# One buffer for a weight chunk's raw words and its low half, and splits two chunks ahead

## The reference

```python
mod = silu(c) @ w_mod[l] + b_mod[l]                    # 6 vectors of 1024: shifts, scales, gates
h = rms_norm(x, g_pre_mix) * (1 + scale1) + shift1
x = x + gate1 * rms_norm(token_mixer(h, ...), g_post_mix)
h = rms_norm(x, g_pre_mlp) * (1 + scale2) + shift2
x = x + gate2 * rms_norm(square(relu(h @ w_ff1)) @ w_ff2, g_post_mlp)
```

## Time and profile before

| | |
|---|---|
| timed runs, median of 3 | 4700.61 us (4700.21 to 4706.22) |
| profiled execution, span | 4705.3 us |
| TensorE busy | 4064.1 us, 86% |
| VectorE busy | 2280.9 us, 48% |
| ScalarE busy | 1600.9 us, 34% |
| weights' low halves (VectorE, L291) | 645 x 1.225 us = 789.1 us |
| weights' high halves (ScalarE, L283) | 645 x 1.055 us = 679.5 us |
| weight loads | 645 x 512 KB, 3.2 us from issue to landing (median) |
| bytes moved by DMA | 356.36 MB, mean 76 GB/s |

### The profile page before, as it was taken

One profiled execution on the slowest core, in us unless ns is written; L12 is line 12 of the kernel. 1 busy time (PEld: TensorE's weight loads), 2 busy tenths in 40 slices (PEclk: granted clock), 3 DMA queues, 4 the chain that ended last, 5 costly groups with the idle time before them and its releaser, 6 DMA issues. The chain is left out here.

```text
span 4705.3 us, 49824 instructions
## 1 busy us (share of the span) xinstructions
PE 4064.1 (86%) x17808; PEld 2981.2 (63%) x17808; DVE 2280.9 (48%) x3743; ACT 1600.9 (34%) x2635; POOL 73.3 (2%) x62
## 2 busy tenths in 40 slices
PE   7879797978899699977978899699979876898877
PEld 5749796733488588756733487588767433685435
DVE  5756564665443444464755443444433345333263
ACT  5445333234433222253334433222222333223332
POOL 0000000010000000000010000000000010000010
PEclk9869898989999799988989999799989578897688
DMA  8305342200022122262200022122222000221001
GB/s 279 126 27 188 121 162 88 85 18 0 18 98 95 51 96 94 85 224 81 85 23 1 18 98 98 50 94 94 84 72 90 0 18 5 72 94 36 14 5 41
DMA packets 95775, 356.36 MB, mean 76 GB/s; under 512 B 11008, under 2 KB 11264, under 8 KB 94592
## 3 DMA queue, kind: packets, MB, share of 16 engines
q1 hardware_dynamic: 95616, 354.27, 21.7%
HBM read 351.08 MB, written 3.15 MB: 75 GB/s over the span
## 5 line engine op out<-in xcount | busy, mean ns | idle before, releaser
L291 DVE TENSOR_TENSOR w_lo<-w_raw,w_hi 128x1024 fp32r<-128x1024 f32 x645 | 789.1, 1225 | 958.4 <-ACT w_hi L283 956.3
L306 PE MATMUL banks<-h_hi,w_hi 128*128 128x512 f32 (+1 forms) x2808 | 1031.5, 367 | 105.3 <-PEq L499 64.1
L307 PE MATMUL banks<-h_lo,w_hi 128*128 128x512 f32 (+1 forms) x2808 | 1027.9, 366 | 0.0
L308 PE MATMUL banks<-h_hi,w_lo 128*128 128x512 f32 (+1 forms) x2808 | 1026.1, 365 | 0.0
L283 ACT ACTIVATE w_hi<-w_raw 128x1024 fp32r<-128x1024 f32 x645 | 679.5, 1055 | 789.0 <-PE banks L308 705.1
L306 PEld LDWEIGHTS banks<-h_hi,w_hi 128*128 128x128 f32 x2808 | 537.3, 191 | 201.5 <-issue 112.3
L307 PEld LDWEIGHTS banks<-h_lo,w_hi 128*128 128x128 f32 x2808 | 537.5, 191 | 89.0
L308 PEld LDWEIGHTS banks<-h_hi,w_lo 128*128 128x128 f32 x2808 | 537.1, 191 | 89.5
L1190 DVE TENSOR_REDUCE row_max<-banks 128x1 f32<-128x768 f32 (+4 forms) x288 | 192.3, 668 | 351.2 <-PE banks L1068 181.7
L1141 ACT ACTIVATE turned<-banks 128x512 f32<-128x512 f32 (+3 forms) x296 | 145.8, 493 | 513.8 <-PE banks L1100 513.1
L1100 PE MATMUL banks<-consts,weights 128*128 128x128 f32 x896 | 187.8, 326 | 127.9 <-DVE weights L1163 83.8
(11 more groups left out here) (255 smaller groups left out, 5213.4 us busy)
## 6 DMA issues: line engine op xcount, KB each, us to landing
w_raw<-in_stream SPq DMA_DIRECT2D x645, 512.0 KB, 3.2
dft_table<-in_dft SPq DMA_DIRECT2D x2, 2048.0 KB, 8.6
x<-in_x SPq DMA_DIRECT2D x1, 2048.0 KB, 11.6
out_x<-x SPq DMA_DIRECT2D x1, 2048.0 KB, 6.3
context<-in_ctx SPq DMA_DIRECT2D x1, 1024.0 KB, 4.6
ctx_kept<-context SPq DMA_DIRECT2D x1, 1024.0 KB, 3.8
rope<-in_rope SPq DMA_DIRECT2D x2, 512.0 KB, 3.6
context<-ctx_kept SPq DMA_DIRECT2D x1, 1024.0 KB, 4.8
```

The costliest lines, as they stand in the source:

```text
L291: self.nc.vector.tensor_tensor(self.lo[:, n % SLOTS], self.raw[:, n % SLOTS], self.hi[:, n % SLOTS].bitcast(F32), ALU.subtract)\
L306: self.nc.tensor.matmul(out, w_hi, x_hi, start=start, stop=False)
L307: self.nc.tensor.matmul(out, w_hi, x_lo, start=False, stop=False)
L308: mm = self.nc.tensor.matmul(out, w_lo, x_hi, start=False, stop=stop)
```

## The change

The low half of a chunk is written over the raw words it was computed from (`over`, with the other type), and the ring `lo` no longer has memory of its own. A load now waits until the products of the chunk in its slot are done, and for nothing else. ScalarE's wait for the used slot goes, because a chunk can't have landed before. `AHEAD` is 2, and SyncE loads up to the stage's end plus 4.

```diff
-AHEAD = 3
+AHEAD = 2
...
         self.raw = K.take("w_raw", [SLOTS, CHUNK * P])
         self.hi = K.take("w_hi", [SLOTS, CHUNK * P], F32R)
-        self.lo = K.take("w_lo", [SLOTS, CHUNK * P], F32R)
+        self.lo = K.over("w_lo", self.raw, F32R)
...
     def load(self, sp, n, place, step=0):
         if n >= SLOTS:
-            sp.wait_ge(self.lo_ready, step + (n - SLOTS + 1))
+            sp.wait_ge(self.chunk_used, step + self.after(n - SLOTS + 1))
...
         act.wait_ge(self.chunk_loaded[n % SLOTS], step_loads + 16 * (n // SLOTS + 1))
-        if n >= SLOTS - 1:
-            act.wait_ge(self.chunk_used, step + self.after(n - SLOTS + 1))
         self.nc.scalar.activation(self.hi[:, n % SLOTS], self.raw[:, n % SLOTS], ACT.Copy)\
             .then_inc(self.hi_ready, 1)
...
+    def over(self, name, t, dt):
+
+        self.n += 1
+        at = next(a for a, _, n in self.held if n == t.name)
+        return self.nc.alloc_sbuf_tensor_at(f"{name}_{self.n}", list(t.shape), dt, offset=at)
+
...
     def _(sp):
-        W.load_upto(sp, end_chunk + AHEAD + SLOTS)
-        W.loaded = min(W.total, end_chunk + AHEAD + SLOTS)
+        W.load_upto(sp, end_chunk + SLOTS)
+        W.loaded = min(W.total, end_chunk + SLOTS)
```

## The result

The changed kernel takes 4738.4 us (median of 4, 4734.9 to 4739.7), the kernel before 4703.3 us in the same comparison: a ratio of 1.0075, 95% interval 1.0063 to 1.0087. The change costs 35 us, where 4717 us, +16.5, had been forecast. It lies in the stated range of 4703 to 4742, near its upper end, and outside the forecast's own 4711 to 4728. The profiled execution spans 4737.0 us against 4705.3.

What follows compares the result with a forecast made beforehand. TensorE was taken to bound the weight stages, except modulation, bound by the weights' slot loop. Modulation +15, gate +1 and SyncE +0.5 gave +16.5 us on the 4705.3 us span, 4721.8; timed runs lie 4.7 lower: 4717 us, range 4703 to 4742.

Steps and rivals of the forecast that it cites:

- Place and mechanism: Modulation stages: the weights' slot loop is the limit there and gets longer by hand-over to TensorE and six matmuls.
- fixed part: Modulation slot loop: everything except a load's issue-to-landing time, 2.58 us before the change and 4.21 us after.
- main term: 22 modulation groups of four chunks go from 7.18 and 7.07 us to 7.8 us: +15 us.
- the bounds: Modulation: landing between 3.2 and 4.6 us, loop 7.41 to 8.81 us, cost +6 to +37 us.
- L: Time from a weight load's issue to its landing in modulation: 4.6 us before, taken as 3.6 us after.
- signs: Modulation: row copies 7.5 to 8.2 us apart, landings 3.2 to 3.8 us, SyncE waiting for matmuls, DMA share about 0.78.
- The lost head start: Seven chunks loaded or split before a stage become four; counted inside the first turn of the loop, nothing extra.
- Rival 1: Modulation: landing doesn't get shorter, staying at 4.6 us; +37 us there, 4739 us in all; chance 0.13.
- The other stages: Outside modulation loads stay hidden: 1 us in the 256-column gate stage, 0.5 us for SyncE at stage ends, otherwise 0.
- Rival 2: Modulation: the slot loop stays under what the DMA engines need; groups stay at 7.1 us, 4701 us; chance 0.23.
- Rival 3: Modulation: TensorE's clock falls to the lower level, groups of 12.2 us, +112 us, 4813 us; chance 0.03.
- Rival 4: Attention: the clock falls otherwise because all is shifted, 10 us either way; chance 0.05 for gain, 0.05 for loss.

Runs made afterwards that it cites:

- wait alone: Changed kernel with separate memory for the low halves, loads still waiting for the products and AHEAD = 2: 4742.5 us, ratio 1.0083.
- AHEAD alone: Kernel before with only AHEAD set from 3 to 2, loads waiting for the low half as before: 4701.3 us, ratio 0.9992.
- one in flight: Changed kernel with SyncE in modulation also waiting for the landing of the load before; one execution, groups of 13.3 us.
- six slots, two in flight: Changed kernel with six slots, SyncE in modulation also waiting for the landing of the load before the last; one execution, groups of 8.75 and 8.61 us.
- six slots: Changed kernel with six slots in place of four and the MLP's loop written out: 4694.7 us against 4701.1 for the kernel before, ratio 0.9982.
- four products: Changed kernel without the products of the condition's low half with the weights' high half in modulation, four matmuls per chunk for six: 4752.5 us, one execution.
- overlay with AHEAD = 3: Changed kernel with AHEAD set from 2 to 3, so chunks are split three ahead: 4786.4 us, ratio 1.0181.
- own ring: Changed kernel with separate low-half memory in the two modulation stages, loads there waiting for the low half as before: 4710.4 us, ratio 1.0014.
- half loads: Changed kernel with separate low-half memory, each modulation load bringing only 512 of 1024 words (results differ): 4707.7 us, one execution.

## Why the prediction was right and wrong

- **Place and mechanism: right.** All of the loss is in modulation, by the slot's loop that now holds TensorE's products. The wait alone makes it, AHEAD alone and writing in place don't. The loop's fixed part was 4.3 us (4.21 forecast).
- **Size of the main term: wrong, 15 us for 37.8.** The step that failed is the one from the bounds to L: "uneven landings add up in a loop in order; I take L = 3.6 and a group of 7.8 us". It leaned on a single row, one load of 3.4 us. What the runs showed is a landing of 4.3 us and groups of 8.48 and 8.76 us, and that the landing grows with every load that is in flight. Loads in flight are 4 L divided by the group's time, GB/s those of a stretch in layer 0:

```
kernel                     group us   landing us   in flight   GB/s
one in flight                13.3        3.2          1.0       158
changed kernel                8.5        4.3          2.0       246
six slots, two in flight      8.7        4.3          2.0       232
before                        7.2        4.6          2.6       290
six slots                     6.7        5.1          3.0       314
```

  The changed kernel's loop could have been closed from rows that were there: from the earlier trace rows (3.2 us, one load in flight) to the earlier trace rows (4.6 us, 2.6 in flight) the landing grows by some 0.9 us per further load. With L = 3.2 + 0.9 (n - 1) and n = 4 L / (L + 4.21) the loop settles at n = 2.0, L = 4.1, a group of 8.3 us: +26 us. This is an estimate made after the fact, and takes the growth as even between two stages. The bounds had been right; the value between them was not worked out, though the loop fixes it. Of the signs that the forecast named for itself only SyncE's wait for matmuls came; copies 7.5 to 8.2 us apart, landings of 3.2 to 3.8 us and a DMA share of 0.78 didn't (8.48 and 8.76, 4.3, 0.73).
- **The rule of the Trainium skill**, "DMA: Bandwidth & Descriptors", section on the anatomy of one DMA, some 2.0 us fixed and the rest by bytes: it is given there for DMAs issued by GpSimd, while these loads are issued by SyncE, and the trace agrees for a lone one (3.2 us for 512 KB). The fit is for one transfer; what the prediction drew from it, that loads 1.9 us apart don't get in each other's way, was wrong by 1.1 us of landing.
- **The lost head start: wrong.** The forecast had it inside the 11 turns, at nothing of its own. Of the 37.8 us 11 x (8.48 - 7.18) + 11 x (8.76 - 7.07) = 32.9 are in the turns and 4.9 outside them. The run with the old wait in modulation shows it apart: 3.0 and 1.0 us outside the groups.
- **Rival 1** (landing doesn't get shorter), given 0.13, came nearest: 4739 us forecast, 4738 measured. That the two agree to 1 us is luck. It had L = 4.6, copies 8.8 us apart and 37 us in the turns; there were 4.3, 8.48 and 8.76, and 32.9, with 4.9 us of head start and an unrelated gain of 6.7 in attention (below) on top. The argument against it, that a slower round means fewer in flight, was true (2.0 for 2.6) and worth only 0.3 us of landing.
- **The range** held because it reached past rival 1, and with some luck: if the timed runs have that gain in attention as the profiled one has, the time without it would be some 4738 + 7 = 4745 us (an estimate), above 4742. The kernel with the wait alone, whose profile doesn't have the gain, took 4742.5 us.
- **The other stages: right.** The 256-column gate stage lost 2.2 us (1 forecast, bound 4), of which 1.8 come with AHEAD = 2 alone; the 512-column gemm lost 0.0. Beside the conv TensorE does run dry and is paced by VectorE. Its timeline there has

```profile
212.25 0.28 PE L306 MATMUL banks<-h_hi,w_lo 128*128 128x256 f32 x1
212.57 0.36 PE L304 MATMUL banks<-h_hi,w_hi 128*128 128x256 f32 x1
...
215.37 0.28 PE L306 MATMUL banks<-h_hi,w_lo 128*128 128x256 f32 x1
215.69 0.36 PE L304 MATMUL banks<-h_hi,w_hi 128*128 128x256 f32 x1
```

  so one chunk every 3.12 us, VectorE's pace in the earlier trace rows, with a start 0.32 us behind the last in place of 0.12; the stage ends no later (83.83 us against 83.97).
- **Rival 2** (the loop isn't the limit) is out: groups got longer. **Rival 3** (the clock falls) did not come in layer 0, where the clock was 1.00; layer 1 shows the edge of it. One group there, from row copy to row copy:

```profile
2056.29:2066.10 9.81, 8.96 (x35) 7.15 (x36) 5.00 (x5) 4.71 (x7) 0.00 (x0) 0.83 0.57 195
```

  Its first products stand in TensorE's timeline as

```profile
2056.53 0.77 PE L1416 MATMUL banks<-w_hi,cond_hi 128*128 128x512 f32 x1 [1.27 <-DVE w_lo L289]
2057.10 0.63 PE L1417 MATMUL banks<-w_hi,cond_lo 128*128 128x512 f32 x1
2057.52 0.63 PE L1418 MATMUL banks<-w_lo,cond_hi 128*128 128x512 f32 x1
```

  so behind a wait of 1.27 us they start 0.43 us apart (the prediction had 0.47 for the lower level). At a mean of 0.83 the group took 9.81 us. The stage's mean was 0.96, and layer 1 lost 2.6 us more than layer 0; how much of that is the clock's isn't shown, since groups at 1.00 took up to 9.37 us. The Trainium skill, "TensorE: Matmul & The Clock Gate", section on HAM oscillation, tells of the clock thrown back by waits for DMA. Here TensorE waited for a low half that had itself waited for its load, and the mean clock was under 1.00 in two groups of layer 1 (0.83 and 0.82) and in 20 of 22 with four products. But not every such wait was followed by a fall: in layer 0 waits of 1.55 and 1.52 us (before 33.75 and 44.35 us) left the clock at 1.00.
- **Rival 4** (attention's clock) came as a gain of 6.7 us in this one profiled execution. Full attention of layer 0 takes either 253.3 to 253.4 us (before, AHEAD alone, overlay with AHEAD = 3, wait alone, own ring, six slots) or 246.3 to 246.7 us (changed, one in flight, two in flight, half loads, four products). That of layer 1 takes 246.2 to 246.9 us in all but one, 249.1 with two in flight. The granted clock goes with it, 0.90 and 0.92. It isn't the change, since kernels with the same wait are in both groups. What decides between the two was not tried and stays open.

## What to carry to other kernels

- Sharing a buffer is a wait moved from the end of a short use to the end of a long one: write down the slot's whole loop, fixed part and landing, and divide by the slots. Where TensorE needs 5.6 us for a chunk it is free; where it needs 1.7 the loop sets the stage's time.
- In a closed loop the landing isn't a free number between two bounds. Take landing against loads in flight from two stretches of the trace and solve for the point at which the loop agrees with itself.
- Memory that an overlay frees is worth more as further slots than as nothing: six shared slots beat four with memory of their own, here by 0.2%.

## What the runs showed of the hardware that was not expected

- A 512 KB load on this core takes 3.2 us alone and, on the mean from one load in flight to three, 0.95 us more for each further one (4.3 at 2.0, 4.6 at 2.6, 5.1 at 3.0), long before the rate is at its highest: 158, 246, 290, 314 GB/s. Two loads in flight don't fill the engines; half the bytes make it 2.8 us at 1.5 in flight.
- Taking a third of TensorE's products out of a stage that waits for loads made the stage longer, 96.3 and 100.0 us for 11 groups against 93.2 and 96.4, with a lower granted clock (0.78 and 0.75 against 1.00 and 0.96). The long groups are those in which the turn of a row fell on the lower level.
